# The order of projections and attention pieces in the dilated block of a two-block model

## The reference

```python
B_GROUPS = ((128, 1), (512, 4), (2048, 16))       # window, dilation
z = h @ w_in                                      # three groups of q, k, v; and a gate
for gi, (window, dil) in enumerate(B_GROUPS):
    # each query sees positions at 0, +-dil, ..., within half a window
    logits = q . k * dh ** -0.5 + bias[bucket(rel * dil)]
    o, lse = softmax(logits) @ v, logsumexp(logits)
wts = softmax(stack(lses), axis=0)                # over the three groups
y = (sum of wts * o) * silu(gate)                 # 16 heads of 64
x = x + rms_norm(y @ w_out)
```

## Time and profile before

| | |
|---|---|
| median of 3 runs | 2633.42 us (2631.6 to 2638.09) |
| the profiled execution | 2640.0 us, its span 2638.3 us |
| TensorE busy, share of the span | 97% |
| VectorE, ScalarE, POOL busy | 64%, 44%, 4% |
| mean granted TensorE clock | 0.99 |
| from issue to landing, median | a weight tile 3.6 us, a bias tile 6.3 us |
| the dilated block's seven calls of the edited function | 533.3 us of the span (2025.46 to 2558.73) |

### The profile page before, as it was taken

The page is one execution under the profiler, slowest core; times in us unless marked ns, Lnnn a source line. Parts: engine busy times, 40 slices in busy tenths (PEclk is TensorE's granted clock), DMA queues, the critical chain, the costliest instruction groups (busy, mean ns, idle before and its releaser), DMA issues. The chain is left out here.

```text
span 2638.3 us, 38406 instructions
## 1 busy us (share of the span) xinstructions
PE 2552.4 (97%) x15278; PEld 2150.9 (82%) x15278; DVE 1689.0 (64%) x2729; ACT 1148.3 (44%) x1975; POOL 109.8 (4%) x125
## 2 busy tenths in 40 slices
PE   7999899999999999999999999999999999999998
PEld 4867788899999978888999988888878777777776
DVE  6567636666666667887888886655665445545455
ACT  3246625433333334655555544322244433434354
POOL 1110001100000000000000000000010000000001
PEclk9999999999999999999999999999989999999999
DMA  6440113433333311112333324332222323323221
GB/s 245 152 134 25 33 49 120 160 112 112 105 106 112 110 42 57 33 49 72 96 113 120 97 86 139 95 92 92 88 76 88 89 82 90 88 67 90 90 90 49
DMA packets 67902, 247.06 MB, mean 94 GB/s; under 512 B 7696, under 2 KB 8240, under 8 KB 67056
## 3 DMA queue, kind: packets, MB, share of 16 engines
q1 hardware_dynamic: 52896, 188.88, 22.8%
q0 software_dynamic: 14688, 55.20, 6.4%
q10 hardware_dynamic: 144, 0.52, 0.1%
HBM read 242.33 MB, written 2.24 MB: 93 GB/s over the span
## 5 line engine op out<-in xcount | busy, mean ns | idle before, releaser
L2853 DVE TENSOR_TENSOR WL<-RAW,WH 128x1024 fp32r<-128x1024 f32 (+1 forms) x193 | 235.6, 1222 | 379.8 <-ACT WH L2045 379.6
L1040 PE MATMUL PS<-AB,BH 128*128 128x384 f32 (+1 forms) x1256 | 387.3, 308 | 4.8 <-DVE BL L2860 3.5
L1040 PE MATMUL PS<-HM,WH 128*128 128x512 f32 x968 | 386.8, 400 | 0.8 <-ACT DG L2045 0.8
L1042 PE MATMUL PS<-AB,BL 128*128 128x384 f32 (+1 forms) x1256 | 385.0, 307 | 0.0
L1041 PE MATMUL PS<-AB,BH 128*128 128x384 f32 (+1 forms) x1256 | 385.0, 306 | 0.0
L1041 PE MATMUL PS<-HM,WH 128*128 128x512 f32 x968 | 378.3, 391 | 0.0
L1042 PE MATMUL PS<-HM,WL 128*128 128x512 f32 x968 | 377.5, 390 | 0.0
L2045 ACT ACTIVATE WH<-RAW 128x1024 fp32r<-128x1024 f32 (+1 forms) x193 | 202.4, 1050 | 257.6 <-PE PS L1042 257.6
L1040 PEld LDWEIGHTS PS<-AB,BH 128*128 128x128 f32 x1256 | 236.0, 188 | 10.5 <-DVE GATED L3363 5.6
L1041 PEld LDWEIGHTS PS<-AB,BH 128*128 128x128 f32 x1256 | 236.0, 188 | 1.1 <-issue 0.5
L1042 PEld LDWEIGHTS PS<-AB,BL 128*128 128x128 f32 x1256 | 235.9, 188 | 0.0
(11 more groups left out here) (461 smaller groups left out, 4936.8 us busy)
## 6 DMA issues: line engine op xcount, KB each, us to landing
RAW<-in_tiles SPq DMA_DIRECT2D x298, 512.0 KB, 3.6
MRAW<-in_mods POOLq DMA_DIRECT2D x80, 512.0 KB, 4.7
RAW_M<-in_tiles SPq DMA_DIRECT2D x34, 512.0 KB, 3.6
TB<-bias_rows POOLq DMA_DIRECT2D x16, 576.0 KB, 6.3
FIRST<-in_mods SPq DMA_DIRECT2D x8, 1024.0 KB, 16.7
X_M<-in_x SPq DMA_DIRECT2D x2, 1024.0 KB, 6.0
VN_GB<-in_gm_rows POOLq DMA_DIRECT2D x2, 1024.0 KB, 6.4
out_x<-X_M SPq DMA_DIRECT2D x8, 256.0 KB, 2.0
```

Of the source, the lines that this page charges most:

```text
L1040: pe.matmul(out_, wh, xh, start=first, stop=False, skip_group_check=True)
L1042: return pe.matmul(out_, wl, xh, start=False, stop=last, skip_group_check=True)
L2853: dve.tensor_tensor(WL[:, s.mod(2), 0:width], RAW[:, s.mod(2), 0:width], f32(WH[:, s.mod(2), 0:width]), ALU.subtract).then_inc(tile_split[ ...
```

## The change

The same calls are made with the same arguments; in the three functions they stand in another order. In the new order TensorE does P0 S0 P1 P2 T0 S1 P3 P4 T1 S2 P5 V0 T2 P6 S3 P7 T3 P8 V1 TV P9. P2 stands directly behind P1, and P4 behind P3. T0 and S1, like T1 and S2 already, stand together between two projections, and so do V1 and TV. The semaphore that each projection waits for is the same as before. ScalarE's and VectorE's orders are changed to agree. The first projections, the last step and the queues of SyncE and POOL are untouched.

```diff
--- before.py
+++ after.py
@@ -1951,22 +1951,22 @@
                 project(p, 0, (dil_qkg_read, q.times(3, 3)))
                 scores(q, 0)
                 project(p, 1, (dil_v_read, p.times(3, 1)))
+                project(p, 2, (dil_v_read, p.times(3, 2)))
                 transposes(q, 0)
-                project(p, 2, (dil_v_read, p.times(3, 2)))
                 scores(q, 1)
                 project(p, 3, (dil_v_read, p.times(3, 3)))
+                project(p, 4, (dil_qkg_read, p.times(3, 1)))
                 transposes(q, 1)
                 scores(q, 2)
-                project(p, 4, (dil_qkg_read, p.times(3, 1)))
+                project(p, 5, (dil_qkg_read, p.times(3, 2)))
                 values(q, 0)
                 transposes(q, 2)
-                project(p, 5, (dil_qkg_read, p.times(3, 2)))
+                project(p, 6, (dil_plain_read, p.times(4, 1)))
                 scores(q, 3)
-                project(p, 6, (dil_plain_read, p.times(4, 1)))
+                project(p, 7, (dil_plain_read, p.times(4, 2)))
                 transposes(q, 3)
-                project(p, 7, (dil_plain_read, p.times(4, 2)))
+                project(p, 8, (dil_score_read, q.times(4, 4)))
                 values(q, 1)
-                project(p, 8, (dil_score_read, q.times(4, 4)))
                 turn_values(p)
                 if p.i is None and p.start == KC - 1:
                     project_freeing(p)
@@ -2734,19 +2734,19 @@
                 taken(p, 0)
                 exps(q, 0)
                 taken(p, 1)
+                taken(p, 2)
                 pts_taken(q, 0)
-                taken(p, 2)
                 exps(q, 1)
                 taken(p, 3)
+                taken(p, 4)
                 pts_taken(q, 1)
                 exps(q, 2)
-                taken(p, 4)
+                taken(p, 5)
                 pts_taken(q, 2)
-                taken(p, 5)
+                taken(p, 6)
                 exps(q, 3)
-                taken(p, 6)
+                taken(p, 7)
                 pts_taken(q, 3)
-                taken(p, 7)
                 taken(p, 8)
                 turned_values(p)
                 if p.i is None and p.start == KC - 1:
@@ -3937,17 +3937,17 @@
                 biased(q, 1)
                 probs(q, 1)
                 read(p, 3)
+                read(p, 4)
                 biased(q, 2)
                 probs(q, 2)
-                read(p, 4)
+                read(p, 5)
                 outs(q, 0)
-                read(p, 5)
+                read(p, 6)
                 biased(q, 3)
                 probs(q, 3)
-                read(p, 6)
                 read(p, 7)
+                read(p, 8)
                 outs(q, 1)
-                read(p, 8)
                 if p.i is None and p.start == KC - 1:
                     kept_chunk(0)
                     for k in range(KC - 1):
```

## The result

| | before | after |
|---|---|---|
| median of 5 runs | 2634.96 us (2631.6 to 2641.75) | 2645.87 us (2638.74 to 2651.56) |
| ratio, 95% interval | | 1.0042 [1.0026, 1.0057] |
| ratio in a second set (8 and 19 runs) | | 1.0029 [1.0014, 1.0043] |
| the seven calls, first S0 to last S0, in the profile | 533.27 us | 540.11 us |
| the second of the seven, S0 to S0 | 76.13 us | 77.29 us |

The change makes the kernel slower by 0.3 to 0.4%. The profiled execution of the changed kernel took 2638.74 us, with a span of 2637.1, less than the one of before; its seven calls are nevertheless 6.84 us longer. The work ahead of the block is the same in both, and the block started 8 us earlier in that execution (2017.69 against 2025.78). So what the change does has to be read inside the block, not from the spans. Seven calls that are 6.84 us longer make a ratio of 1.0026.

A forecast was written before the change was run, and what follows sets the result against it. TensorE, busy 97% of the span, was taken as the bound. Stretches of +0.45 and +6.28 less 5.53 gave +1.20 us a step, times seven +8.4, on 2633.4: 2641.8 us, range 2635.5 to 2647.

The forecast's parts named there:

- The stall at P2: Between P1 and P2, TensorE waits for ScalarE's copy of P1 out of bank 7: 1.38 to 1.48 us, taken as 1.46.
- The stall at P4: Between P3 and P4, TensorE waits for VectorE's gate operation to read bank 7: 1.79 to 1.89 us, taken as 1.84.
- The chain: Ahead of P4: probs(q, 1), P3's end, tanh, gate; times from P2's last matmul, tanh starting at 8.81 us.
- The stretches: P1's last matmul to S1's first, 8.01 to 8.46 us; P3's last to V0's first, 9.58 to 15.86 us.
- the end: After V0, the old P8 between V1 and TV falls out: 5.53 us less a step.
- T to S: From a T's first matmul to the next S without a wait: 1.46 us, bounded by 1.23 and 1.65.
- The last call: The seventh call of the edited function, costed at the same +1.20 us as each other step.
- T0's and T1's waits: Behind two projections, their waits of 0.6 to 0.7 us ahead and up to 0.3 us inside go.
- T3's wait: Stays, with one projection between S3 and T3; a rival, chance 0.08, has it fall too, leaving +0.2 us a step.
- the late gate: Rival, chance 0.12: P3's gate stays late, P4 stalls 2.36 us, +1.72 us a step, 2645.5 us.
- Faster: Rival, chance 0.06: no bank 7 stalls, gaps 0.23 us at P2 and P4, -1.64 us a step, 2622 us.
- The clock: Rival, chance 0.04: stalls lower TensorE's clock, one projection a step at half clock costs 39 us in all, 2672 us.

The follow-up runs named there:

- after_again: The changed kernel measured once more, unedited; ratio to the kernel before 1.0029, seven calls 540.34 us.
- values_only: The kernel before with only V1 moved behind P8; one run, seven calls 531.58 us against 533.27.
- half_early: The kernel before with only P2 moved ahead of T0; ratio to before 0.9983, seven calls 529.04 us.
- best: banks_both with T3 also behind two projections in the six calls ahead of the last; ratio to before 0.9947, seven calls 518.33 us.
- banks_both: The changed kernel with P2 and P4 in PSUM bank 3 instead of 7, plus the needed waits; ratio to before 0.9952, seven calls 520.31 us.
- half_late: The changed kernel without the move of P2; ratio to the kernel before 1.0056, seven calls 549.46 us.
- bank_p2: The changed kernel with P2 alone in PSUM bank 3; one run, seven calls 531.10 us.
- copy_first: The changed kernel with ScalarE's taken(p, 1) put ahead of exps(q, 0); one run, seven calls 537.90 us.

## Why the prediction was right

The direction and the mechanism held, and two sizes were helped by luck. The forecast was +8.4 us; the medians say +10.9 and, in the second set, +8.6 (2644.18 - 2635.62); the traces say +6.84 in the seven calls. The 4 us between the first pair of medians and the traces are not shown to come from anything; the traces' 1.0026 is the lower end of that interval and lies inside the second. The forecast itself gave "slower" a chance of 0.51, and the second set, at 0.29%, lies on the edge that it named.

By its steps:
- The stall at P2: 1.46 forecast, 1.38 to 1.47 measured (the prediction's own terms, with the release of 0.15 that it names, give 1.48). The place of exps(q, 0) is 0.30 of it, where the prediction's 0.75 less 0.42 is 0.33.
- The stall at P4: 1.84 forecast, 1.89 measured. The chain came as worked out: from P2's last matmul probs(q, 1) ends at 8.72 (8.73 forecast), P3's last matmul is at 8.32 (8.39), the tanh starts at 8.74 (8.81).
- The stretches: 8.40 against 8.46, 15.86 against 15.86, the end 5.53 less as forecast. T to S is 1.40 and not 1.46; in the second stretch this miss and the 0.05 us that P4's stall is longer cancel, so that the exact 15.86 is luck. A step is 1.14 us longer (77.26 against 76.12, mean of the first six without the third, in which the kernel before lost another 0.3 us at the loop's jump; the changed kernel lost nothing there in this profile, and 0.3 us in that of after_again, so that this is scatter), +1.20 forecast.
- The last call was taken like the others. It lost only 0.35 us (76.56 against 76.21), since the first part's wait for HM shrank by 0.8 us (values_only). With the 0.3 us of the third step and the 0.06 of each, this is the distance between 8.4 and 6.84.
- T0's and T1's waits went, but the reason given, "behind two projections", is wrong for T1. half_early shows that its wait goes with the move of P2. The sum was right because both waits were taken out once. That is the step of the working that was wrong: the gain at T1 was booked to the pair P3 P4, and it hid that the second pair is pure loss: with the shift of the later runs it costs 1.72 us a step on top of half_early (77.29 against 75.57), and P2's move without it is a gain.
- T3's wait was read from one call, 0.91 us behind P6. In the other calls of the kernel before it is 0.84 to 1.19, five times 1.1 us or more. The price of 1.0 us a step for all of it was right all the same: best takes it away, and its step is 0.99 us shorter than that of banks_both.

The rivals: the late gate is what happens without P2's move (2.44 us in half_late), and not with it. "Faster" needed both gaps under 2.10 us together; they are 3.27. T3's wait did not fall. The clock did not fall behind 1.38 and 1.89 us (1.00 over the block), but it did behind 2.44, in five of seven calls: that rival was nearer than its chance of 0.04 says. One of the five runs of the changed kernel has a mean granted clock of 0.94 on record, the others 0.988 to 0.991; no trace of it is kept, its time is the median, and what lowered the clock stays open. The Trainium skill's warning (TensorE: Matmul & The Clock Gate, A second HAM failure mode: psum-queue depth-cycling) fits half_late and not the two traces of the changed kernel.

## What to carry to other kernels

Before two accumulations are put next to one another, look at the bank that the second one writes: the reader's latency that other work covered becomes a stall of its full length, here 1.4 us for a copy and 1.9 for a tanh with an operation of another engine behind it, together more than the waits that the move took away. Take the parts of a reordering one by one: here one half gained, one lost, and a bank that was free at that time turned a loss of 0.3% into a gain of 0.5%. And compare stages, not spans, where the change is smaller than the scatter of the work ahead of it.

## What was not expected of the hardware

After a stall of 2.44 us, behind 5.3 us of matmuls, the granted clock fell to the lower level (0.52 in the window shown) in five of seven cases, 1.6 us each; after stalls of 1.89 us it never did in the fourteen calls of the two profiles of the changed kernel, and not in the fourteen of bank_p2 and copy_first. What decides between the five calls and the two of half_late is not shown. The jump back of TensorE's loop costs nothing to 0.3 us where a whole projection stands directly ahead of it (the third step: 76.45 in the kernel before, against 76.12; 77.25 in the changed one, against 77.26; 77.54 in after_again), and 2.1 us of idle time plus 1.6 us of slower matmuls where values and twelve transposes stand between the last projection and the jump (best).
